# DSA logits and index products from fp32r halves, and another order of the dense work beside three attentions

## What is computed

```python
def second_block(x, ...):
    h = rmsnorm_2(x, norm_g[l])
    (q_lat, c_kv, k_rope, z_a, q_b, k_b, v_b, z_b,
     q_idx, k_idx, w_idx, gate_a, gate_b) = jnp.split(h @ w_in[l], cuts, axis=-1)
    ...
    y_a = mla_attention(...) * jax.nn.silu(z_a)
    y_b = dsa_attention(...) * jax.nn.silu(z_b)
    merged = (jax.nn.sigmoid(gate_a) * (y_a @ w_o_a[l])
              + jax.nn.sigmoid(gate_b) * (y_b @ w_o_b[l]))
    x = x + merged @ w_out[l]

def dsa_block(...):
    s = jnp.einsum('bqhd,bkd->bqhk', qi, k_idx) * (IDX_DIM ** -0.5)      # 8 index heads of 32
    score = jnp.einsum('bqhk,bqh->bqk', jax.nn.relu(s), wi * (IDX_HEADS ** -0.5))
    score = jnp.where(admissible[None], score, -jnp.inf)
    _, idx = lax.top_k(score, topk)                                      # 128 keys of 512 for each query
    logits = jnp.einsum('bqhd,bqkhd->bhqk', qb, gather(k, idx)) * scale  # 8 heads of 64
    logits = logits + bias by relative position, masked
    p = jax.nn.softmax(logits, axis=-1)
    return jnp.einsum('bhqk,bqkhd->bqhd', p, gather(v, idx))
```

## Time and profile before

| | us |
|---|---|
| median of 3 runs (1153.26 to 1154.55) | 1153.38 |
| the profiled execution | 1154.94 |
| its span | 1153.2 |
| TensorE busy (5149 passes) | 1093.9 |
| VectorE busy | 625.8 |
| ScalarE busy | 449.1 |
| POOL busy | 261.1 |
| a weight load, issue to landing, median of 164 | 3.4 |

### The profile page before, as it was taken

How to read it: one execution, slowest core, us unless ns; L and a number is a source line. 1 busy time by engine, 2 the same in 40 slices (tenths; PEclk the granted TensorE clock), 3 DMA queues, 4 the chain that set the end, 5 groups by cost and what they waited for, 6 DMA issues and landing times.

```text
span 1153.2 us, 13400 instructions
## 1 busy us (share of the span) xinstructions
PE 1093.9 (95%) x5149; PEld 846.5 (73%) x5156; DVE 625.8 (54%) x1058; ACT 449.1 (39%) x767; POOL 261.1 (23%) x158
## 2 busy tenths in 40 slices
PE   7799989979999999999999999888999999999995
PEld 5596777747888888888888755666886666788884
DVE  5756565647444422444445458877666544225544
ACT  6634354546322311232244555244434444323332
POOL 0672322302110100011024123211331232321101
PEclk9899989989999999999999999989999999999998
DMA  7031222212322232222322312211212222232321
GB/s 281 20 111 37 70 85 87 75 37 74 106 96 95 92 123 91 91 93 92 102 100 91 112 34 82 71 69 68 91 55 74 74 74 71 72 104 92 108 93 73
DMA packets 31215, 99.87 MB, mean 87 GB/s; under 512 B 3768, under 2 KB 4424, under 8 KB 31152
## 3 DMA queue, kind: packets, MB, share of 16 engines
q1 hardware_dynamic: 31152, 99.02, 25.7%
HBM read 94.38 MB, written 4.72 MB: 86 GB/s over the span
## 4 chain that ended last, share of the span: by engine, by line
PE 77%; DVE 11%; ACT 5%; issue 3%; DMA 2%; SPq 1%; POOL 0%; DVEq 0%; ACTq 0%; POOLq 0%
PE bank L1234 21%; PE bank L1235 20%; PE bank L1236 20%; DMA WS<-wall 2%; PE bank L1364 2%; PE bank L1342 2%; PE bank L1355 2%; PE bank L1246 1%; PE bank L1248 1%; PE bank L1247 1%; SPq L1198 1%; DVE m L1868 1%; DVE score L1870 1%; ACT WH L1402 1%; DVE score L1859 1%
## 5 line engine op out<-in xcount | busy, mean ns | idle before, releaser
L1234 PE MATMUL bank<-HH,WH 128*128 128x512 f32 x808 | 329.8, 408 | 16.1 <-DVE WL L1631 8.3
L1236 PE MATMUL bank<-HH,WL 128*128 128x512 f32 x808 | 317.3, 393 | 0.0
L1235 PE MATMUL bank<-HL,WH 128*128 128x512 f32 x808 | 316.8, 392 | 0.0
L1939 POOL TENSOR_TENSOR WL<-WS,WH 128x1024 fp32r<-128x1024 f32 x64 | 154.2, 2409 | 391.3 <-ACT WH L1402 390.7
L1234 PEld LDWEIGHTS bank<-HH,WH 128*128 128x128 f32 x808 | 153.7, 190 | 60.6 <-issue 14.0
L1402 ACT ACTIVATE WH<-WS 128x1024 fp32r<-128x1024 f32 x164 | 170.6, 1047 | 64.2 <-PE bank L1236 42.6
L1236 PEld LDWEIGHTS bank<-HH,WL 128*128 128x128 f32 x808 | 152.8, 189 | 33.0
L1235 PEld LDWEIGHTS bank<-HL,WH 128*128 128x128 f32 x808 | 153.3, 190 | 29.2 <-issue 1.0
L1631 DVE TENSOR_TENSOR WL<-WS,WH 128x1024 fp32r<-128x1024 f32 x100 | 132.7, 1332 | 30.0 <-ACT WH L1402 30.0
L1992 POOL TENSOR_TENSOR fa<-fa,fg 128x512 f32<-128x512 f32 x22 | 28.3, 1287 | 273.4 <-DVE fa L1821 273.4
L1234 PE MATMUL bank<-GH,WH 128*128 128x512 f32 x176 | 68.5, 389 | 0.0
(11 more groups left out here) (314 smaller groups left out, 1717.8 us busy)
## 6 DMA issues: line engine op xcount, KB each, us to landing
WS<-wall SPq DMA_DIRECT2D x164, 512.0 KB, 3.4
scratch<-scratch SPq DMA_DIRECT2D x8, 317.5 KB
X<-xT SPq DMA_DIRECT2D x8, 256.0 KB, 6.8
b_t<-scratch SPq DMA_DIRECT2D x8, 256.0 KB, 3.9
outT<-X SPq DMA_DIRECT2D x5, 256.0 KB, 2.3
f_s<-f_s SPq DMA_DIRECT2D x8, 128.0 KB
f_m<-f_m SPq DMA_DIRECT2D x8, 128.0 KB
outT<-o_x SPq DMA_DIRECT2D x3, 256.0 KB, 2.0
```

The costliest lines, as they stand in the source:

```text
L1234: e.matmul(b[:, :], wh, xh[:, at_k, :], start=k == 0, stop=False)
L1235: e.matmul(b[:, :], wh, xl[:, at_k, :], start=False, stop=False)
L1236: m = e.matmul(b[:, :], wl, xh[:, at_k, :], start=False, stop=k == n - 1)
L1939: e.tensor_tensor(WL[:, u % NW, :], WS[:, u % NST, :], f32(WH[:, u % NW, :]), ALU.subtract).then_inc(*tick(w_low_g, u))
```

## The change

DSA's q and k become stacks like Fox's: for each head a stationary operand b_s1 of 128 rows (64 high, 64 low of q) and two moving ones, b_m1 (high of k, twice) and b_m2 (low of k, twice), in three slots; SP copies the halves of k across. Logits of a block are two fp32r passes and the mask. For the index products, q of a head is stacked as high, low, high of 32 rows and the keys as high, high, low, so that one fp32r pass of 96 rows makes a product; 24 DMAs of 32 rows carry q there. The three first DSA pairs' products and gates go in between MLA's, DSA's pairs begin one by one as their stack, gate and the masks are there, and the rates change.

```diff
-        i_k = sub("i_k", [128, T], F32, 6)
+        i_kk = sub("i_kk", [96, T], F32R, 6)
+        i_qh = sub("i_qh", [128, 2, T], F32R, 68)
+        i_ql = sub("i_ql", [128, 2, T], F32R, 72)
+        i_qq = [sub(f"i_qq{i}", [96, T], F32R, o) for i, o in enumerate((84, 86, 88, 90, 92, 80, 82, 44))]
...
-        b_qk = [sub(f"b_qk{i}", [128, 2, T], F32, 16 + 4 * i) for i in range(2)]
+        sq0, sq1 = (at(f"sq{i}_late", [128, T], F32R, o) for i, o in enumerate(sq_at))
+        b_s1 = [sub("b_s10", [128, T], F32R, 16), sub("b_s11", [128, T], F32R, 22), sub("b_s12", [128, T], F32R, 56)]
+        b_m1 = [sub("b_m10", [128, T], F32R, 18), sq1, sub("b_m12", [128, T], F32R, 64)]
+        b_m2 = [sub("b_m20", [128, T], F32R, 20), sub("b_m21", [128, T], F32R, 2), sq0]
+        b_st = [[sqb[0], sub("b_st0", [128, T], F32, 2)], [sub("b_st1", [128, T], F32, 58), sub("b_st2", [128, T], F32, 52)],
+                [sub("b_st3", [128, T], F32, 58), sub("b_st4", [128, T], F32, 66)]]
...
-              fox_side(), 0.8)
+              fox_side(), 0.62)
...
+        do("index_keys")
+        for j in range(2):
+            do("index_stack", j=j)
...
-        now["per"] = 1.1
+        now["per"] = 1.4
...
-        for _ in range(6):
+        for _ in range(9):
...
+        def dsa_stack(p):
+            for n in range(5):
+                hl, what = n // 2, "qk"[n % 2]
+                if n < 4:
+                    if what == "q":
+                        while not slot_ring.ready():
+                            yield
+                        i, _, free = slot_ring.take()
+                        slot_of[2 * p + hl] = i, free
+                    i, free = slot_of[2 * p + hl]
+                    do("bstack_high", p=p, hl=hl, what=what, i=i, free=free)
+                if n > 0:
+                    hl, what = (n - 1) // 2, "qk"[(n - 1) % 2]
+                    i, free = slot_of[2 * p + hl]
+                    do("bstack_low", p=p, hl=hl, what=what, i=i, free=free)
+                if n == 4:
+                    dsa_in[p] = True
+                yield
         def dsa_products(p):
-            while not b_ring.ready():
+            while (p == 1 and ("logits", ("mla", 5, 3)) not in known) or (p == 2 and ("logits", ("mla", 7, 3)) not in known) \
+                    or (p >= 2 and p - 1 not in dsa_in):
                 yield "not yet"
-            i, qk, free = b_ring.take()
+            free = [[total_g(("lq", 2)), idx_p((1, 7))], [logits(("mla", 5, 3))], [logits(("mla", 7, 3))], []][p]
+            st = b_st[min(p, 2)]
             yield from product(f"qb{p}", "w_in_2", 0, cols(P_QB + 128 * p), "h3", NK,
-                               scaled(f"qb{p}", qk[:, 0, :], 0.125, norm=n3, free=[free, dense("uq7")]))
+                               scaled(f"qb{p}", st[0][:, :], 0.125, norm=n3, free=free))
             yield from product(f"kb{p}", "w_in_2", 0, cols(P_KB + 128 * p), "h3", NK,
-                               scaled(f"kb{p}", qk[:, 1, :], 1.0, norm=n3, free=[free, dense("uq7")]))
-            dsa_in[p] = i, qk
-            yield from z_products("zb", P_ZB, p)
+                               scaled(f"kb{p}", st[1][:, :], 1.0, norm=n3, free=free))
+            behind.append(dsa_stack(p))
 
...
+        ga_ring = Ring(acc)
+        ga_at = {}
+        def gate_a(m):
+            ga_at[m] = ga_ring.take()
+            yield from gate(m, "ga", P_GA, ga_at[m])
+        def gated_ya(m):
+            yield from gated(m, "ga", "w_o_a_2", "ya", ga_at[m], a_half[m], None)
+            ga_ring.give(ga_at[m][0], out_v(("oga", m)))
 
         def mla_side():
             for p in range(1, 4):
                 do("copy_rows", heads=(2 * p, 2 * p + 1))
-                yield from mla_products(p)
+            yield from mla_products(1)
+            yield from dsa_products(0)
+            yield from mla_products(2)
+            yield from gate_a(0)
+            yield from mla_products(3)
             yield from dsa_v()
             dsa_bias(0)
-            for p in range(4):
-                yield from dsa_products(p)
-            assert ("ya", 3) in known
-            ga_ring = Ring(acc)
-            for m in range(8):
-                g = ga_ring.take()
-                yield from gate_pair(m, "ga", "w_o_a_2", P_GA, "ya", g, a_half[m], None)
-                ga_ring.give(g[0], out_v(("oga", m)))
-        def dsa_ready():
-            if 0 not in dsa_in or "zb0" not in gates:
-                return False
-            if behind and next(behind[0], "end") == "end":
+            yield from z_products("zb", P_ZB, 0)
+            yield from dsa_products(1)
+            yield from gated_ya(0)
+            yield from z_products("zb", P_ZB, 1)
+            yield from dsa_products(2)
+            yield from gate_a(1)
+            yield from gated_ya(1)
+            yield from dsa_products(3)
+            yield from z_products("zb", P_ZB, 2)
+            for m in range(2, 8):
+                yield from gate_a(m)
+                yield from gated_ya(m)
+                if m == 3:
+                    yield from z_products("zb", P_ZB, 3)
+        def dsa_ready(p):
+            if (p not in dsa_in or "masks" not in known) and behind and next(behind[0], "end") == "end":
                 behind.pop(0)
-            return not behind
+            return p in dsa_in and "masks" in known and f"zb{p}" in gates
 
...
+                elif kind == "bstack_high" and s["what"] == "k":
+                    i, hl = s["i"], s["hl"]
+                    hd, r, o = 2 * s["p"] + hl, slice(64 * hl, 64 * hl + 64), slice(64 - 64 * hl, 128 - 64 * hl)
+                    q.wait_ge(bstack_a(("k", hd)))
+                    e.dma_start(f32(b_m1[i][o, :]), f32(b_m1[i][r, :])).then_inc(*bstack_in[i].tick())
+                elif kind == "bstack_low" and s["what"] == "k":
+                    i, hl = s["i"], s["hl"]
+                    hd, r, o = 2 * s["p"] + hl, slice(64 * hl, 64 * hl + 64), slice(64 - 64 * hl, 128 - 64 * hl)
+                    q.wait_ge(bstack_v(("k", hd)))
+                    e.dma_start(f32(b_m2[i][o, :]), f32(b_m2[i][r, :])).then_inc(*bstack_in[i].tick(hd))
...
-                elif kind == "keys":
-                    q.wait_ge(out_v("is"))
-                    for g in range(4):
-                        e.dma_start(i_k[32 * g:32 * g + 32, :], i_s[0:32, :]).then_inc(*keys_in.tick())
+                elif kind == "index_stack":
+                    j = s["j"]
+                    for h in range(4):
+                        r, dst = slice(32 * h, 32 * h + 32), i_qq[4 * j + h]
+                        q.wait_ge(istack_a(("q", j)))
+                        e.dma_start(f32(dst[0:32, 128:T]), f32(i_qh[r, j, 128:T])).then_inc(*index_in[j].tick())
+                        e.dma_start(f32(dst[64:96, 128:T]), f32(i_qh[r, j, 128:T])).then_inc(*index_in[j].tick())
+                    for h in range(4):
+                        r, dst = slice(32 * h, 32 * h + 32), i_qq[4 * j + h]
+                        q.wait_ge(istack_v(("q", j)))
+                        e.dma_start(f32(dst[32:64, 128:T]), f32(i_ql[r, j, 128:T])).then_inc(*index_in[j].tick())
...
-                        q.wait_ge(out_v(f"kb{hd // 2}"), s["free"])
-                        e.matmul(b[:, 0:n], s["qk"][r, 0, qs], s["qk"][r, 1, 0:n], start=True, stop=False)
+                        at_i = s["qk"]
+                        q.wait_ge(bstack_v(("k", hd)), bstack_in[at_i](hd), s["free"])
+                        e.matmul(b[:, 0:n], b_s1[at_i][:, qs], b_m1[at_i][:, 0:n], start=True, stop=False)
+                        e.matmul(b[:, 0:n], b_s1[at_i][:, qs], b_m2[at_i][:, 0:n], start=False, stop=False)
                         if i == 0:
...
-                    r, n = slice(32 * (hd % 4), 32 * (hd % 4) + 32), 128 * (i + 1)
-                    q.wait_ge(keys_in(), out_v(f"qi{hd // 4}"), s["free"])
-                    e.matmul(s["b"][:, 0:n], i_q[r, hd // 4, i * 128:i * 128 + 128], i_k[r, 0:n], start=True,
+                    n = 128 * (i + 1)
+                    q.wait_ge(istack_v("k"), index_in[hd // 4](), s["free"])
+                    e.matmul(s["b"][:, 0:n], i_qq[hd][:, i * 128:i * 128 + 128], i_kk[:, 0:n], start=True,
...
+                elif kind == "bstack_low":
+                    i, hl, what, st = s["i"], s["hl"], s["what"], b_st[min(s["p"], 2)]
+                    hd, r, o = 2 * s["p"] + hl, slice(64 * hl, 64 * hl + 64), slice(64 - 64 * hl, 128 - 64 * hl)
+                    q.wait_ge(bstack_a((what, hd)), s["free"], dense("uq7"))
+                    if what == "q":
+                        e.tensor_tensor(b_s1[i][o, :], st[0][r, :], f32(b_s1[i][r, :]), ALU.subtract).then_inc(
+                            *bstack_v.tick((what, hd)))
+                    else:
+                        e.tensor_tensor(b_m2[i][r, :], st[1][r, :], f32(b_m1[i][r, :]), ALU.subtract).then_inc(
+                            *bstack_v.tick((what, hd)))
```

(24 more changed lines are left out.)

47 lines of the change are left out of this document (36 added, 11 removed).

## The result

The changed kernel takes 1195.53 us in the median (1194.3 to 1198.18), the kernel before beside it 1153.97: 1.0357 times as long (95% interval 1.0328 to 1.0386), some 42 us more. The forecast was 1180, with a range of 1160 to 1196.

The account below looks back on a forecast made before the run. TensorE was taken as the bound nearly everywhere, with room at Fox's end and in MLA. Terms -12.8 - 7 + 10 + 40.3 - 4 = +26.5 us on 1154.94 gave 1181.4, set to 1180 us by the median; range 1160 to 1196.

Parts of the forecast that it names:

- Sign: Whole kernel: the change makes it slower, chance 0.86, against 0.10 for faster and 0.04 for same.
- The six copies: MLA: six scratch-row copies issued back to back before uk1 act serially, 79.6 us without weights; +40.3 us.
- The stand: MLA: one stretch without TensorE work of about 40 us from near 770 us, while ScalarE's split waits for a load.
- Rival 1: MLA row copies: they don't add up, as loads slip between or engines differ; faster, 1135 us; chance 0.08.
- DSA logits: DSA attention: 32 products fall from 24.3 to 11.5 us as two fp32r passes each, all of it counting; -12.8 us.
- MLA's rest: MLA after the copies: dense work is all but never refused; -4 us, ends 0 and -12.
- Sum +10 us; ends -5 and +15: Fox attention at rate 0.62 for 0.8: fuller end -9.5, later stacks 16.5 more waiting, lower clock 3 more.
- The three waits: Fox, pairs 1, 2 and 3: TensorE waits 7.5, 3.6 and 8.5 us for stack copies, 16.5 us more than before.
- the gain at the end: End of Fox: later dense steps cut the loss there from 12 us to 2.5; -9.5 us.
- Index: Index products: 24 products fall from 20.3 to 4.3 us on TensorE, little passes through; -7 us, ends -4 and -12.
- the load that was to set the pace: Index part: unit 107's weight load behind the first pair of row copies lands 26.4 us after issue, blocking ScalarE's split.

Follow-up runs that it names:

- e3: The kernel before with each row copy issued as 112 and 15 rows: 1151.72 us, 0.9953 of the kernel before.
- e10: The changed kernel with the two fp32r passes of each DSA logits product made twice: 1205.69 us.
- e12: The kernel before with row copies of 112 and 15 rows and Fox's rate 0.8 for 40 main steps, then 0.35: 1144.9 us, 0.9903.
- e2: The changed kernel with each row copy issued as 112 and 15 rows, in the same place: 1155.63 us, 0.9991 of the kernel before.
- e9: The changed kernel with row copies of 112 and 15 rows and Fox's rate 0.8 for 40 main steps, then 0.35: 1130.1 us, 0.9782.
- e5: The changed kernel, rate still 0.62, with two steps of stack work behind each dense step of Fox in place of one: 1186.33 us.
- e11: The changed kernel with 21 of VectorE's 24 score operations on 64 columns in place of 256 to 512: 1193.28 us.
- e7: The changed kernel with the index weights turned three dense steps earlier, ahead of the bias rows: 1197.06 us.

## Why the prediction was right or wrong

- **Sign, order and range**: right. But 1195.5 lies half a microsecond inside the upper end of the range, two of the four executions lie above it (1196.57 and 1198.18), and it is 42 us for the 26.5 forecast. That the median is still inside is luck: two terms came out 14 us too high together.
- **The six copies** (+40.3): right in mechanism and place, and close in size. 12.5 us each, 79.55 us from issue to split, resumed at X + 85.84. Spreading them gives 40.8 us, but 4.3 of that the kernel before lost as well (e3), so against it the six cost 36.5. The stand was foretold from near 770 and came at 789, mostly because Fox and the index part end 14 us later than was forecast.
- **Rival 1**, copies that don't add up, is out: they add up to the microsecond.
- **DSA logits** (-12.8): the durations are right, or better at 128 columns. Close to nine tenths of what was added in e10 is seen; of the 14.1 us by the rows ((0.76 - 0.32) * 32) that makes 12.4, an estimate.
- **MLA's rest** (-4): not measured alone. With spread copies on both sides, the stretch from uk0 to the end falls from 424.4 (e3) or 425.8 (e12) to 410.3 (e2, e9), so DSA and MLA together give 14.1 to 15.5 where 16.8 was forecast. Less the estimate for DSA this leaves some 2 to 3. That the whole stretch came out within 1 us is in part two misses that cancel: the copies cost 2 to 4 less than forecast, DSA and MLA gave 1 to 3 less.
- **Fox, "Sum +10 us; ends -5 and +15"**: this is the step that failed, by 8.7 us and beyond its end. The three waits were put at 7.5, 3.6 and 8.5 and measured 8.45, 6.03 and 9.26, so 4 us of it are theirs. Some 24 dense passes run at the lower clock, 0.43 for 0.227 us, which is 4.8 us and not 3. With 20.8 us more waiting and 4.6 more at the lower clock than before, the sum of 18.65 leaves 7 for the gain at the end, where 9.5 was taken; the 7 is a remainder and wasn't measured by itself. All three were sized on the friendly side, and the end of +15 with them. The prediction counted how much later a stack is asked for; it passed over that pair 3's products themselves end only just ahead, so that what is in front of the copies can't be hidden (12.7 us in e5, 10.6 of them a wait). The seam itself moves by some 3 us with the same code (last section), which doesn't bring it inside: at 661.62, the earliest, the loss is still over 15.
- **Index, "TensorE gains 16.0, but little passes through ... -7"**: failed by 5.4 us. The first score was put at 4 us later for three dense steps; it came 9 later. The products of the bias rows (1.24 us in all, at 687.28), which before stood behind the first scores, and the 2.6 us wait for ScalarE's bias rows now come ahead of it, and neither was counted. And the load that was to set the pace is only 1.8 us of it; with no wait for it (e2) nothing is gained. What does set the pace stays open, as said above.

## What to carry to other kernels

A DMA that is "off the path" is still in somebody's queue: count what one costs the queue, multiply by how many are issued in a row, and compare it with the stock that the queue keeps filled. Two copies at a time were all but free in the changed kernel (4 to 5 us in the kernel before), and six cost 40 us; a row count that divides well made all six nearly free. When dense work is spread to last to an end, look first at which of it produces operands: those steps belong early, and only the rest may be thinned out, which here was worth 25 us against a rate of 0.62 throughout and 3 to 7 against 0.8. And a faster product moves the pace to the next engine's queue, so its saving is read from the waits that are left, one change at a time and then together.

## What was not expected

- VectorE's operations on tensors stop for GpSimd's. In e11 a score over 64 columns takes 0.28 us alone, and 2.2 when it starts beside a WL of GpSimd. GpSimd's and then VectorE's timeline in e11 (two scores are in the 2.49):

```profile
709.20 2.38 POOL L2055 TENSOR_TENSOR WL<-WS,WH 128x1024 fp32r<-128x1024 f32 x1 [5.64 <-ACT WH L1483]
...
729.59 2.36 POOL L2055 TENSOR_TENSOR WL<-WS,WH 128x1024 fp32r<-128x1024 f32 x1 [5.01 <-ACT WH L1483]
```

```profile
709.57 2.49 DVE L1975 SCALAR_TENSOR_TENSOR score<-sq,wi,score 128x64 f32<-128x64 f32 x2 [5.16 <-ACT sq L1673]
712.39 0.28 DVE L1975 SCALAR_TENSOR_TENSOR score<-sq,wi,score 128x64 f32<-128x64 f32 x1 [0.34 <-ACT sq L1673]
...
729.86 2.17 DVE L1975 SCALAR_TENSOR_TENSOR score<-sq,wi,score 128x64 f32<-128x64 f32 x1 [1.63 <-ACT sq L1673]
```

  The last ends with GpSimd's, at 732.0, whatever its own length. A score with one tensor input does so too: 2.35 us at 716.40 for 384 columns, beside a WL from 716.13, against 0.58 for 512 columns at 696.18. The Trainium skill (SBUF — State Buffer, SBUF: two separate sides) says that the two engines hold a common pair of ports exclusively for a whole instruction; the trace agrees. The 1157 ns of the earlier trace rows is thus a mean of 0.69 and 2.5 us, and in Fox the slow kind stood in the stack's chain of two of the three waits.
- The same code takes different times up to the end of Fox. The seam at 664.24 us lies at 661.62 in e7 and at 667.52 in e2, which have nothing changed ahead of it, and the difference is carried to the end. So a few microseconds between two profiled executions are read between two seams, not from the spans. What makes it stays open.
